# Issuing each weight block's load one block ahead in a streaming-encoder layer on eight cores

## The chip, the cores and the metric

The kernel runs on one Trainium2 chip as one program on 8 cores. Each core gets one half of one of four prompt sequences and two of sixteen short sample sequences; the cores exchange nothing. The metric is the device time of the slowest core in microseconds (us), as the median over runs.

## The reference, cut to what matters

One transformer-like layer with two parallel head groups. For every token of width 1024:

```python
h = rms_norm(x) * (1 + scale1) + shift1
z = h @ w_in                                  # 1024 x 3584, seven blocks of 512 columns
qa, ka, va, qr, kr, vr, gr = split(z)         # blocks 0, 1, 2, 3, 4, 5, 6
qa, ka = rms_norm per 64 columns
qr, kr = rotate(qr, pos), rotate(kr, pos)     # rotary tables
oa  = diff_attention(qa, ka, va)              # 4 heads, two softmax maps, 64-token causal chunks
orr = retention_scan(qr, kr, vr) * silu(gr)   # 4 heads, recurrent state
x = x + gate1 * (concat(oa, orr) @ w_out)     # two blocks of 512 columns
h2 = rms_norm(x) * (1 + scale2) + shift2
x = x + gate2 * ((silu(h2 @ w_gate) * (h2 @ w_up)) @ w_down)   # 11 blocks up, 6 blocks down
```

Outputs are the new `x` for prompt and sample, the normalised keys, the values and the final retention states. The prompt has 8192 tokens per sequence, the sample 32 tokens on top of a cache of 2048.

## The kernel before, in words

The program is written out by Python. Each operation is appended to the list of its engine together with the buffers that it reads and writes; the semaphores that an instruction waits for follow from these. Nothing is reordered: each engine, and each of the two queues that issue transfers, works through its list in program order. All loads into on-chip memory come from the SP queue (helper `ld`), all stores to HBM and all casting loads from the POOL queue (`stq`). So a load on SP that has to wait for its buffer holds up every load behind it.

The prompt is done in eight steps of two tiles of 512 tokens: the **foreign** tile, which the core only needs for keys, values and state, and the **own** tile, for which it computes everything. `in_proj` multiplies a tile by blocks of `w_in`. For the foreign tile the blocks are 1, 2, 4, 5, here called F1, F2, F4, F5; for the own tile they are 1, 2, 0, 4, 5, 3, 6, here called O1, O2, O0, O4, O5, O3, O6. A block has four groups of 8 matmuls (128 tokens each) that go to four PSUM banks in turn, and each group is then read out by VectorE (DVE) or ScalarE (ACT): blocks 0 and 1 by a norm (`qknorm`), blocks 3 and 4 by a rotation (`rope`, six DVE operations), blocks 2 and 5 by copies that alternate between ACT and DVE. After F1's matmuls the hook `own_norm` loads the own tile's `x` (`s_xo`) and normalises it: ACT squares and sums, DVE writes `s_xn`. A block's transposes are put off until after the next block's matmuls.

Weights go through `wring`, a ring of three slots of 1 MB. `load_w` takes the next slot, and its load waits for the last matmul that read the slot's former block (three blocks earlier). In the source the load stands at the head of its own block. Rotary tables (`s_rt`, two buffers of 512 KB) are loaded in blocks 3 and 4, one per group, so the third and the fourth of such a block wait for the first and the second `rope` of that block. Attention loads keys and values (`s_ktb`, `s_vsb`) in pairs of 128 KB through two buffers.

A step goes: F blocks, store of the foreign keys and values, state update, transposes of the own tile, O blocks (`kp`, `vp` are stored from one buffer each, four times), retention, attention over all earlier tiles (so later steps are longer), output projection (`Wo`), norm, feed-forward (`Wgu` eleven blocks, `Wd` six), with the next foreign tile's norm hooked into it. The last stage does the sample with 64 tokens.

Weights arrive in 32-bit floats and are cast once into 16-bit scratch in HBM by the POOL queue: `Wi` at the very start, `Wo`, `Wgu`, `Wd` in the middle of the first step (`prepass_rest`).

Of the kernel before, what the change touches and what calls it, by code (L numbers as in the profile page):

```python
# [294 lines left out]
def build_program(n_steps=NT // 2, do_sample=True, cut=0):  # L295
    def chk(n):
        if cut == n:
            raise _StopBuild()
# [32 lines left out]
    rope_d = din("rope", [NT, TT, 4, 256])  # L331
# [16 lines left out]
    Wi = dscr("Wi", [7, 128, 8, 512], BF16)  # L348
# [156 lines left out]
    def load_w(src, nk, ncol, rkeys):  # L505
        view, key = wslot(nk, ncol)
        ld(view, src, r=rkeys, w=[key])
        return view, key

    def setup():  # L510
        ld(kc[:], kc_d[:], w=["kc"])
        ld(dco[:], dco_d[:], w=["dco"])
# [213 lines left out]
                else:  # L726
                    act(dest[:, h, 0:T], tbb[:, half * 512:half * 512 + T], AF.Copy, [tk], [(dname, h)])

    def in_proj(rows, nsub, own, sample, tabsrc, tile_i, hook_after_first=None):
        T = rows * nsub  # L730
        hk_ = hT_keys(sample)
        cbs = (1, 2, 0, 4, 5, 3, 6) if own else (1, 2, 4, 5)
        pending = [None]

        def flush():
            if pending[0] is not None:
                pending[0]()
                pending[0] = None
        for cb in cbs:
            W, wkey = load_w(Wi[cb], 8, 512, [("Wi", cb)])  # L740
            if cb == 6:
                for e in range(4):
                    acc, ak = next_acc()
                    for k in range(8):
                        mm(acc[:, 0:T], W[:, k, e * 128:(e + 1) * 128], hT[:, k, 0:T], k == 0, k == 7, [wkey] + hk_, [ak])
                    act(sgT[:, e, 0:T], acc[:, 0:T], AF.Silu, [ak], [("sgT", e)])
                flush()
                continue
            for s in range(nsub):
                acc, ak = next_acc()  # L750
                for k in range(8):
                    mm(acc[0:rows, :], hT[:, k, s * rows:(s + 1) * rows], W[:, k, :], k == 0, k == 7, [wkey] + hk_, [ak])
                chk(31)
                if cb == 0:
                    qknorm(acc, ak, rows, 0, tokb[0:rows, s, :], ("tokb", s), s % 2)
                elif cb == 1:
                    if own:
                        kfv = kf[0:rows, 0, :]
                        qknorm(acc, ak, rows, 64, kfv, "kf", s % 2)
                        if sample:  # L760
                            out_ops.append(stq(ksm[:, :], kfv, r=["kf"]))
                        else:
                            out_ops.append(stq(kp[tile_i, s * 128:(s + 1) * 128, :], kfv, r=["kf"]))
                        act(tokb[0:rows, s, :], kfv, AF.Copy, ["kf"], [("tokb", s)])
                    else:
                        qknorm(acc, ak, rows, 64, tokb[0:rows, s, :], ("tokb", s), s % 2)
                elif cb == 2:
                    if own:
                        vfv = vf[0:rows, 0, :]
                        act(vfv, acc[0:rows, :], AF.Copy, [ak], ["vf"])  # L770
                        if sample:
                            out_ops.append(stq(vsm[:, :], vfv, r=["vf"]))
                        else:
                            out_ops.append(stq(vp[tile_i, s * 128:(s + 1) * 128, :], vfv, r=["vf"]))
                        cp(vst[0:rows, s, :], vfv, ["vf"], [("vst", s)])
                    else:
                        evac(vst[0:rows, s, :], acc[0:rows, :], [ak], [("vst", s)])
                elif cb in (3, 4):
                    rs_ = s % 2
                    ld(rt[0:rows, rs_], tabsrc(s), w=[("rt", rs_)])  # L780
                    if cb == 3:
                        rope(acc, ak, rows, rt[0:rows, rs_, 0, :], rt[0:rows, rs_, 1, :], ("rt", rs_), tokb[0:rows, s, :], ("tokb", s), s % 2)
                    else:
                        rope(acc, ak, rows, rt[0:rows, rs_, 2, :], rt[0:rows, rs_, 3, :], ("rt", rs_), ke[0:rows, s, :], ("ke", s), s % 2)
                elif cb == 5:
                    evac(vR[0:rows, s, :], acc[0:rows, :], [ak], [("vR", s)])
            if hook_after_first is not None and cb == cbs[0]:
                hook_after_first()
            flush()
            if cb == 0:  # L790
                pending[0] = lambda: transp_heads(tokb, lambda s: [("tokb", s)], rows, nsub, qAT, "qAT", split=True)
            elif cb == 1:
                pending[0] = lambda: transp_heads(tokb, lambda s: [("tokb", s)], rows, nsub, kst, "kst")
            elif cb == 3:
                pending[0] = lambda: transp_heads(tokb, lambda s: [("tokb", s)], rows, nsub, qdT, "qdT")
            elif cb == 4 and own:
                pending[0] = lambda: transp_heads(ke, lambda s: [("ke", s)], rows, nsub, keT, "keT")
        flush()
# [164 lines left out]
    def out_proj(rows, nsub, xviews, xkeys):  # L963
        okeys = [("oT", i) for i in range(8)]
        for cb2 in range(2):
            W, wkey = load_w(Wo[cb2], 8, 512, [("Wo", cb2)])
            for s in range(nsub):
                acc, ak = next_acc()
                for k in range(8):
                    mm(acc[0:rows, :], oT[:, k, s * rows:(s + 1) * rows], W[:, k, :], k == 0, k == 7, [wkey] + okeys, [ak])  # L970
                t = et[0:rows, (cb2 * nsub + s) % 2, :]
                tkey = f"et{(cb2 * nsub + s) % 2}"
                tt(t, acc[0:rows, :], gate1b[0:rows, cb2 * 512:(cb2 + 1) * 512], ALU.mult, [ak, ("gate", 0, cb2)], [tkey])
                xv = xviews[s][:, cb2 * 512:(cb2 + 1) * 512]
                tt(xv, t, xv, ALU.add, [tkey, xkeys[s]], [xkeys[s]])

    def ffn(rows, nsub, xviews, xkeys, sample, store, gb_hooks=None, mid_hook=None):
        T = rows * nsub
        hk_ = hT_keys(sample)
        for gb in range(11):  # L980
            W, wkey = load_w(Wgu[gb], 8, 512, [("Wgu", gb, 0), ("Wgu", gb, 1)])
            if gb_hooks is not None and gb in gb_hooks:
                gb_hooks[gb]()
            for fc in range(2):
                pg, pgk = next_acc()
                pu, puk = next_acc()
                for k in range(8):
                    mm(pg[:, 0:T], W[:, k, fc * 128:(fc + 1) * 128], hT[:, k, 0:T], k == 0, k == 7, [wkey] + hk_, [pgk])
                for k in range(8):
                    mm(pu[:, 0:T], W[:, k, 256 + fc * 128:256 + (fc + 1) * 128], hT[:, k, 0:T], k == 0, k == 7, [wkey] + hk_, [puk])  # L990
                sgi = (2 * gb + fc) % 2
                sg = lg[:, sgi, 0:T]
                act(sg, pg[:, 0:T], AF.Silu, [pgk], [("lg", sgi)])
                tt(ffT[:, 2 * gb + fc, 0:T], pu[:, 0:T], sg, ALU.mult, [puk, ("lg", sgi)], [("ffT", 2 * gb + fc)])
# [5 lines left out]
        for half in range(2):  # L1000
            accs = [next_acc() for s in range(nsub)]
            for bi, (k0, k1) in enumerate(((0, 8), (8, 16), (16, 22))):
                W, wkey = load_w(Wd[half][:, k0:k1, :], k1 - k0, 512, [("Wd", half, bi)])
                for s in range(nsub):
                    acc, ak = accs[s]
                    for kk in range(k0, k1):
                        mm(acc[0:rows, :], ffT[:, kk, s * rows:(s + 1) * rows], W[:, kk - k0, :], kk == 0, kk == NKF - 1, [wkey] + fkeys, [ak])
# [33 lines left out]
    try:  # L1041
# [14 lines left out]
        for step in range(n_steps):  # L1056
# [5 lines left out]
                    ld(xviews[s], xs[slotO, s * 128:(s + 1) * 128, :], w=[xkeys[s]])  # L1062
                norm_part(xviews, xkeys, 128, [0, 1, 2, 3], 0)
            chk(1)
            in_proj(128, 4, False, False, lambda s, slot=slotF: rope_d[slot, s * 128:(s + 1) * 128], step, hook_after_first=own_norm)
            chk(2)
            store_kv(slotF)
            pu, pk = psb[7], PS(7)
# [21 lines left out]
            for h in range(4):  # L1090
                ts(tmpS[:, h, :], S[:, h, :], dco[:, 8 + h:9 + h], None, ALU.mult, None, ["S", "dco"], [("tmpS", h)])
                stt(tmpS[:, h, :], Uf[:, h, :], dco[:, 16 + h:17 + h], tmpS[:, h, :], ALU.mult, ALU.add, ["Uf", "dco", ("tmpS", h)], [("tmpS", h)])
                stt(S[:, h, :], pu[:, h * 128:(h + 1) * 128], dco[:, 12 + h:13 + h], tmpS[:, h, :], ALU.mult, ALU.add, [pk, "dco", ("tmpS", h)], ["S"])
            chk(6)
            for h in range(4):
                attention(0, 512, prompt_units(step, h), h)
            chk(7)
# [7 lines left out]
            if step + 1 < n_steps:  # L1105
                nslot = 2 * (step + 1)
                ffn(128, 4, xviews, xkeys, False, store,
                    gb_hooks={1 + 2 * s_: (lambda nslot=nslot, s_=s_: foreign_sub(nslot, s_)) for s_ in range(4)}, mid_hook=foreign_part2)
            else:
                ffn(128, 4, xviews, xkeys, False, store)  # L1110
        out_ops.append(stq(rp[:].rearrange("h d e -> d h e"), S[:, :, :], r=["S"]))
# [135 lines left out]
```

How the kernel before makes its waits and increments, by code:

```python
        def run_engine(e, h):  # L151
            seen = {}
            nwait = 0
            for o in prog.ops[e]:
                need = {}
                for d in o.deps:
                    if (not d.is_dma) and d.eng == e and e == "pe" and not o.is_dma:
                        continue
                    k = d.sem
                    if d.val > seen.get(k, 0) and d.val > need.get(k, 0):
                        need[k] = d.val
                for k, v in need.items():
                    h.wait_ge(sem_h[k], v)
                    seen[k] = v
                    nwait += 1
                ins = o.fn(h)
                if o.is_dma:
                    ins.then_inc(sem_h[o.sem], 16)
                elif o.signal:
                    ins.then_inc(sem_h[o.sem], 1)
            if e == "sp":
                for k, v in cnt.items():
                    h.wait_ge(sem_h[k], v)
            prog.stats["n_wait"][e] = nwait
```

## Time and profile before

| | |
|---|---|
| median of 2 runs | 5278.8 us (5278.3 to 5279.2) |
| profiled execution, time | 5300.7 us |
| its span on the slowest core (core 5) | 5299.1 us |
| spans of the eight cores | 5268.3 to 5299.1 us |
| mean granted TensorE clock of the cores | 0.888 to 0.897 |
| TensorE (PE) matmul busy | 4040.6 us, 76% |
| ACT busy | 2372.2 us, 45% |
| DVE busy | 1278.3 us, 24% |

How to read it: busy time is the sum of instruction durations on the slowest core. A granted clock of 1.0 is 2.4 GHz and 0.5 is 1.2 GHz. A wait is put down to whichever of the awaited events came last; a load's time is from issue to landing. The timelines of two engines have the same zero, so that a row of SP can be laid beside a row of PE.

### The profile page before, as it was taken

To read this page: it belongs to the slowest core of one execution; us is meant where nothing else is said; L and a number is where in the kernel's file an instruction comes from. 1 tells how busy PE (TensorE), PEld (TensorE's weight loads), DVE (VectorE), ACT (ScalarE), POOL (GpSimd) and SP (SyncE) were. 2 spreads that over 40 slices of the span, in tenths; PEclk is the share of its full clock that TensorE was granted. 3 is DMA by queue.
4 is the path that set the end of the run, shared out by engine and by line. 5 is a ranking of instruction groups with operands and counts; after the bars stand their busy time and mean duration, and the time that the engine had idled before them with its cause. 6 is when DMAs were issued, how large, how long until landed. Compare 5 with 4: busy or idle time off the path is not lost.

```text
span 5299.1 us, 62757 instructions; the slowest of 8 cores (5268.3 to 5299.1 us)
## 1 busy us (share of the span) xinstructions
PE 4040.6 (76%) x19438; PEld 1734.8 (33%) x19438; DVE 1278.3 (24%) x2668; ACT 2372.2 (45%) x3571; POOL 201.5 (4%) x289
## 2 busy tenths in 40 slices
PE   1557966886888688967898688985898966989854
PEld 1223422332333233422333233332333422333323
DVE  0233242233223311242023311133101242001111
ACT  0225324523652366335752367622677324776033
POOL 1010010000000000010000000000000010000000
PEclk8778987998899899988999889998899988999956
DMA  9689551244125412351125411254111452112545
GB/s 120 151 152 142 166 150 46 94 165 131 29 92 172 130 32 68 136 178 44 40 93 170 130 32 41 90 170 139 31 42 59 139 159 72 42 40 66 144 118 180
DMA packets 248993, 556.28 MB, mean 105 GB/s; under 512 B 38660, under 2 KB 180171, under 8 KB 216928
## 3 DMA queue, kind: packets, MB, share of 16 engines
q1 hardware_dynamic: 156240, 444.51, 25.7%
q0 software_dynamic: 92432, 107.77, 11.8%
q8 instruction: 168, 2.75, 0.2%
q14 instruction: 153, 1.25, 0.1%
HBM read 548.22 MB, written 86.78 MB: 120 GB/s over the span
## 4 chain that ended last, share of the span: by engine, by line
PE 59%; DMA 12%; ACT 12%; DVE 9%; issue 8%; DVEq 0%; ACTq 0%; SPq 0%; POOL 0%; POOLq 0%
PE psall L433 58%; DMA s_wring<-Wi 4%; DVE s_et L448 4%; ACT s_Pm L444 3%; ACT s_hT L444 2%; ACT s_et L444 2%; ACT s_lg L444 1%; DMA vp<-s_vf 1%; DMA kp<-s_kf 1%; DVE s_stat L688 1%; DMA Wi<-w_in 1%; ACT s_sqb L444 1%; ACT s_stat L444 1%; DMA y<-s_xo 1%; PE psall L440 1%
## 5 line engine op out<-in xcount | busy, mean ns | idle before, releaser
L444 ACT ACTIVATE s_Pm<-psall,s_cols 128x1024 bf16<-128x1024 f32 (+4 forms) x1332 | 1223.8, 926 | 417.9 <-PE psall L433 376.1
L433 PE MATMUL psall<-s_wring,s_hT 128*128 128x512 bf16 (+1 forms) x2608 | 680.7, 422 | 421.3 <-DMA s_wring<-Wi 202.3
L433 PE MATMUL psall<-s_Pm,s_vsb 128*128 128x512 bf16 (+4 forms) x2560 | 729.0, 354 | 201.9 <-ACT s_Pm L444 145.6
L433 PE MATMUL psall<-s_hT,s_wring 128*128 128x512 bf16 (+1 forms) x3456 | 725.4, 376 | 110.0 <-DMA s_wring<-Wi 67.2
L433 PE MATMUL psall<-s_qAT,s_ktb 128*128 128x512 bf16 (+4 forms) x2560 | 701.6, 359 | 28.7 <-ACT s_et L444 26.0
L433 PE MATMUL psall<-s_Pm,s_onesb 128*128 128x512 bf16 (+5 forms) x2576 | 702.4, 354 | 20.9 <-DVE s_S L456 19.0
L433 PEld LDWEIGHTS psall<-s_wring,s_hT 128*128 128x128 bf16 (+1 forms) x2608 | 269.3, 106 | 811.1 <-issue 586.4
L433 PEld LDWEIGHTS psall<-s_hT,s_wring 128*128 128x128 bf16 x3456 | 327.4, 103 | 505.9 <-issue 175.3
L433 PEld LDWEIGHTS psall<-s_Pm,s_vsb 128*128 128x128 bf16 x2560 | 186.5, 97 | 675.0 <-issue 659.7
L456 DVE SCALAR_TENSOR_TENSOR s_lg<-psall,s_G 128x128 f32<-128x128 f32 x120 | 31.5, 292 | 1415.5 <-PE psall L433 1414.9
L433 PEld LDWEIGHTS psall<-s_qAT,s_ktb 128*128 128x128 bf16 x2560 | 243.0, 99 | 306.4 <-issue 51.8
L433 PEld LDWEIGHTS psall<-s_Pm,s_onesb 128*128 128x128 bf16 (+1 forms) x2576 | 240.2, 98 | 272.8 <-issue 37.7
L444 ACT ACTIVATE s_lg<-psall 128x512 f32<-128x512 f32 (+2 forms) x238 | 144.4, 607 | 409.6 <-PE psall L433 408.9
L433 PE MATMUL psall<-s_wring,s_ffT 128*128 128x512 bf16 (+1 forms) x1452 | 322.0, 384 | 5.7 <-DMA s_wring<-Wd 4.6
L448 DVE TENSOR_TENSOR s_ffT<-psall,s_lg 128x512 bf16<-128x512 f32 (+1 forms) x198 | 126.7, 640 | 543.5 <-PE psall L433 410.2
L433 PE MATMUL psall<-s_warmb,s_onesb 128*128 128x512 bf16 x1008 | 224.6, 380 | 0.0
L444 ACT ACT_TABLE_LOAD x94 | 120.6, 1283 | 201.3 <-PE psall L433 184.1
L444 ACT ACTIVATE s_et<-psall 128x512 f32<-128x512 f32 (+2 forms) x106 | 59.1, 558 | 323.7 <-PE psall L433 279.9
L433 PEld LDWEIGHTS psall<-s_wring,s_ffT 128*128 128x128 bf16 (+1 forms) x1452 | 143.5, 99 | 180.9 <-issue 16.8
L448 DVE TENSOR_TENSOR s_et<-psall,s_rt 128x256 f32<-128x256 f32 (+1 forms) x392 | 165.6, 422 | 129.2 <-DMA s_rt<-rope 73.7
L444 ACT ACTIVATE s_Pm<-s_lg 128x128 bf16<-128x128 f32 (+3 forms) x408 | 138.5, 350 | 82.7 <-DVE s_lg L456 52.9
L444 ACT ACTIVATE s_hT<-psall,s_modc 128x512 bf16<-128x512 bf16 (+1 forms) x224 | 141.7, 727 | 72.8 <-PE psall L440 71.3
(158 smaller groups left out, 2632.8 us busy)
## 6 DMA issues: line engine op xcount, KB each, us to landing
s_wring<-Wgu SPq DMA_DIRECT2D x99, 1024.0 KB, 5.9
s_wring<-Wi SPq DMA_DIRECT2D x95, 1024.0 KB, 7.8
s_rt<-rope SPq DMA_DIRECT2D x96, 512.0 KB, 5.9
s_ktb<-KT SPq DMA_DIRECT2D x288, 128.0 KB, 2.0
s_vsb<-VS SPq DMA_DIRECT2D x288, 128.0 KB, 2.0
s_wring<-Wd SPq DMA_DIRECT2D x36, 1024.0 KB, 4.9
s_wring<-Wo SPq DMA_DIRECT2D x18, 1024.0 KB, 7.8
s_wring<-w_ada POOLq DMA_DIRECT2D x16, 1024.0 KB, 12.4
```

The lines of the kernel that those rows point to most:

```text
L433: return P.op("pe", lambda e: e.matmul(out, lhsT=lhsT, rhs=rhs, start=start, stop=stop), reads=r, writes=w)
L440: return P.op("pe", lambda e: e.transpose(out, in_, ident), reads=r, writes=w)
L444: return P.op("act", lambda e: e.activation(out=out, in_=in_, func=func, bias=bias, scale=scale), reads=r, writes=w)
L448: return P.op(eng, lambda e: e.tensor_tensor(out=out, in0=in0, in1=in1, op=op), reads=r, writes=w)
L456: return P.op("dve", lambda e: e.scalar_tensor_tensor(out=out, in0=in0, scalar=scalar, in1=in1, op0=op0, op1=op1), reads=r, writes=w)
L688: P.op("dve", lambda e: e.tensor_reduce(out=stat[0:rows, sc:sc + 8], in_=sq.rearrange("p (g j) -> p g j", g=8), axis=AX.X, op=ALU.add), re ...
```

## The change

`load_w` is split in two. A table `WSRC` names the source of each weight block; `prefetch(name)` issues the load into the next ring slot and keeps the view in `pf`, and `get_w(name)` hands that view out, or loads on the spot if there is none. In `in_proj` and `ffn` each block first gets its own weights and then prefetches the next block's, before any other load of the block; the last block prefetches the first of what comes next where the caller names it (`next_w`). Before attention the three blocks `Wo` 0, `Wo` 1 and `Wgu` 0 are prefetched. The ring keeps its three slots, and the engines PE, DVE, ACT and POOL keep their instructions and their order.

```diff
+    def prefetch(name):
+        if name not in pf:
+            pf[name] = load_w(*WSRC[name])
+
+    def get_w(name):
+        if name in pf:
+            return pf.pop(name)
+        return load_w(*WSRC[name])
...
-        for cb in cbs:
-            W, wkey = load_w(Wi[cb], 8, 512, [("Wi", cb)])
+        for ci, cb in enumerate(cbs):
+            W, wkey = get_w(("Wi", cb))
+            if ci + 1 < len(cbs):
+                prefetch(("Wi", cbs[ci + 1]))
+            elif next_w is not None:
+                prefetch(next_w)
...
-            W, wkey = load_w(Wo[cb2], 8, 512, [("Wo", cb2)])
+            W, wkey = get_w(("Wo", cb2))
...
-            W, wkey = load_w(Wgu[gb], 8, 512, [("Wgu", gb, 0), ("Wgu", gb, 1)])
+            W, wkey = get_w(("Wgu", gb))
+            prefetch(("Wgu", gb + 1) if gb + 1 < 11 else ("Wd", 0, 0))
...
-                W, wkey = load_w(Wd[half][:, k0:k1, :], k1 - k0, 512, [("Wd", half, bi)])
+                W, wkey = get_w(("Wd", half, bi))
+                nxt = ("Wd", half, bi + 1) if bi < 2 else (("Wd", 1, 0) if half == 0 else next_w)
+                if nxt is not None:
+                    prefetch(nxt)
...
+            prefetch(("Wo", 0))
+            prefetch(("Wo", 1))
+            prefetch(("Wgu", 0))
             for h in range(4):
                 attention(0, 512, prompt_units(step, h), h)
```

Where this moves loads is seen in the SP queue. Its list for the first step, from F1 to the first loads of attention, before the change (`s_wring<-Wi` is a block of `w_in`, `s_xo<-xs` the own tile, `s_rt<-rope` a rotary table; the third row from the end is O6's load):

```order
L462 DMA s_wring<-Wi 128x4096
L462 DMA s_xo<-xs 128x1024 x4
L462 DMA s_wring<-Wi 128x4096 x2
L462 DMA s_rt<-rope 128x1024 x4
L462 DMA s_wring<-Wi 128x4096 x5
L462 DMA s_rt<-rope 128x1024 x4
L462 DMA s_wring<-Wi 128x4096 x2
L462 DMA s_rt<-rope 128x1024 x4
L462 DMA s_wring<-Wi 128x4096
L462 DMA s_ktb<-KT 128x512
L462 DMA s_vsb<-VS 128x512
```

The same stretch of the SP queue with the change:

```order
L462 DMA s_wring<-Wi 128x4096 x2
L462 DMA s_xo<-xs 128x1024 x4
L462 DMA s_wring<-Wi 128x4096 x2
L462 DMA s_rt<-rope 128x1024 x4
L462 DMA s_wring<-Wi 128x4096 x5
L462 DMA s_rt<-rope 128x1024 x4
L462 DMA s_wring<-Wi 128x4096 x2
L462 DMA s_rt<-rope 128x1024 x4
L462 DMA s_wring<-Wo 128x4096 x2
L462 DMA s_wring<-Wgu 128x4096
L462 DMA s_ktb<-KT 128x512
L462 DMA s_vsb<-VS 128x512
```

Every weight load has moved up by one place among the weight loads: F2 now stands ahead of the four `x` loads, F5 ahead of F4's four tables, O5 ahead of O4's, and O6 ahead of O3's. The three blocks that are needed after attention stand ahead of its first key and value loads.

## Rows read from the trace of the kernel before

**Rows 1.** The page: the span and the engines' busy times.

```profile
span 5299.1 us, 62757 instructions; the slowest of 8 cores (5268.3 to 5299.1 us)
PE 4040.6 (76%) x19438; PEld 1734.8 (33%) x19438; DVE 1278.3 (24%) x2668; ACT 2372.2 (45%) x3571; POOL 201.5 (4%) x289
```

**Rows 2.** Waits of PE, whole span: who for whom, us in total, times, longest.

```profile
PE psall L433 <- DMA s_wring<-Wi: 269.5, 25, 18.6
PE psall L433 <- DVE s_et L448: 195.2, 84, 12.6
...
PE psall L433 <- DMA s_wring<-Wgu: 15.0, 8, 4.2
```

**Rows 3.** Timeline of PE, fifth step, F1 to F5: start, us, idle before.

```profile
2871.82 7.07 PE L433 MATMUL psall<-s_wring,s_hT 128*128 128x512 bf16 x32
2890.35 8.79 PE L433 MATMUL psall<-s_wring,s_hT 128*128 128x512 bf16 x32 [11.46 <-DMA s_wring<-Wi]
...
2899.87 7.07 PE L433 MATMUL psall<-s_wring,s_hT 128*128 128x512 bf16 x32
2916.86 9.18 PE L433 MATMUL psall<-s_wring,s_hT 128*128 128x512 bf16 x32 [9.93 <-DMA s_wring<-Wi]
```

**Rows 4.** Timeline of PE, same step, end of O4 to the transposes after O6.

```profile
2986.29 1.06 PE L440 MATMUL psall<-s_identb,s_tokb 128*128 128x128 bf16 x16
2999.75 8.70 PE L433 MATMUL psall<-s_wring,s_hT 128*128 128x512 bf16 x32 [12.40 <-DMA s_wring<-Wi]
...
3009.18 7.07 PE L433 MATMUL psall<-s_wring,s_hT 128*128 128x512 bf16 x32
3024.95 9.74 PE L433 MATMUL psall<-s_hT,s_wring 128*128 128x512 bf16 x32 [8.70 <-DMA s_wring<-Wi]
3034.53 1.06 PE L440 MATMUL psall<-s_identb,s_tokb 128*128 128x128 bf16 x16
```

**Rows 5.** Timeline of the SP queue, same step: first issue, us to the last, count.

```profile
2873.37 8.61 SPq L462 DMA_DIRECT2D s_xo<-xs  x4
2882.13 0.80 SPq L462 DMA_DIRECT2D s_wring<-Wi  x2
2882.98 24.86 SPq L462 DMA_DIRECT2D s_rt<-rope  x4
2907.99 35.57 SPq L462 DMA_DIRECT2D s_wring<-Wi  x5
2943.71 46.97 SPq L462 DMA_DIRECT2D s_rt<-rope  x4
2990.83 0.80 SPq L462 DMA_DIRECT2D s_wring<-Wi  x2
```

**Rows 6.** Timeline of DVE, same step: F1's last norm, own norm, O4's first ropes.

```profile
2887.10 0.69 DVE L448 TENSOR_TENSOR s_tokb<-s_et,s_gfull 128x512 bf16<-128x512 f32 x1
2891.75 2.74 DVE L452 TENSOR_SCALAR s_xn<-s_xo,s_stat 128x1024 bf16<-128x1024 f32 x4 [3.96 <-ACT s_stat L444]
...
2985.14 0.95 DVE L448 TENSOR_TENSOR s_et<-psall,s_rt 128x256 f32<-128x256 f32 x2
...
2987.92 0.95 DVE L448 TENSOR_TENSOR s_et<-psall,s_rt 128x256 f32<-128x256 f32 x2
```

**Rows 7.** Transfers of the whole span: issuer, count, KB each, median us to landing.

```profile
s_rt<-rope SPq DMA_DIRECT2D x96, 512.0 KB, 5.9
...
vp<-s_vf POOLq DMA_DIRECT2D x32, 256.0 KB, 2.3
```

**Rows 8.** Chain of waits, fifth step: the second of O1's key stores.

```profile
2946.47 7.26 DMA kp<-s_kf
```

**Rows 9.** First step: PE's waits up to 470 us; POOL's casting of Wgu.

```profile
PE psall L433 <- DMA s_wring<-Wi: 34.0, 2, 18.6
...
345.27 0.83 POOL L465 DMA_DIRECT2D Wgu<-wu  x1 [4.30 <-DMA Wgu<-wu]
```

**Rows 10.** Fifth step by stretch: us, busy times, granted clock, DMA share, GB/s.

```profile
2934.00:2987.00 53.00, 36.12 (x157) 15.07 (x158) 19.52 (x32) 14.82 (x37) 11.79 (x18) 0.86 0.43 111
```

More of the change, by code:

```diff
@@ L508, in load_w @@
         return view, key
+    pf = {}
+    WSRC = {}
+    for cb_ in range(7):
+        WSRC[("Wi", cb_)] = (Wi[cb_], 8, 512, [("Wi", cb_)])
+    for cb_ in range(2):
+        WSRC[("Wo", cb_)] = (Wo[cb_], 8, 512, [("Wo", cb_)])
+    for gb_ in range(11):
+        WSRC[("Wgu", gb_)] = (Wgu[gb_], 8, 512, [("Wgu", gb_, 0), ("Wgu", gb_, 1)])
+    for half_ in range(2):
+        for bi_, (k0_, k1_) in enumerate(((0, 8), (8, 16), (16, 22))):
+            WSRC[("Wd", half_, bi_)] = (Wd[half_][:, k0_:k1_, :], k1_ - k0_, 512, [("Wd", half_, bi_)])
+    def prefetch(name):
[5 more added lines that the diff above has]
+        return load_w(*WSRC[name])
     def setup():
@@ L727, in transp_heads, with in_proj @@
                     act(dest[:, h, 0:T], tbb[:, half * 512:half * 512 + T], AF.Copy, [tk], [(dname, h)])
-    def in_proj(rows, nsub, own, sample, tabsrc, tile_i, hook_after_first=None):
+    def in_proj(rows, nsub, own, sample, tabsrc, tile_i, hook_after_first=None, next_w=None):
         T = rows * nsub
@@ L975, in out_proj, with ffn @@
                 tt(xv, t, xv, ALU.add, [tkey, xkeys[s]], [xkeys[s]])
-    def ffn(rows, nsub, xviews, xkeys, sample, store, gb_hooks=None, mid_hook=None):
+    def ffn(rows, nsub, xviews, xkeys, sample, store, gb_hooks=None, mid_hook=None, next_w=None):
         T = rows * nsub
@@ L1064, in build_program @@
             chk(1)
-            in_proj(128, 4, False, False, lambda s, slot=slotF: rope_d[slot, s * 128:(s + 1) * 128], step, hook_after_first=own_norm)
+            in_proj(128, 4, False, False, lambda s, slot=slotF: rope_d[slot, s * 128:(s + 1) * 128], step, hook_after_first=own_norm, next_w=("Wi", 1))
             chk(2)
@@ L1107, in build_program @@
                 ffn(128, 4, xviews, xkeys, False, store,
-                    gb_hooks={1 + 2 * s_: (lambda nslot=nslot, s_=s_: foreign_sub(nslot, s_)) for s_ in range(4)}, mid_hook=foreign_part2)
+                    gb_hooks={1 + 2 * s_: (lambda nslot=nslot, s_=s_: foreign_sub(nslot, s_)) for s_ in range(4)}, mid_hook=foreign_part2,
+                    next_w=("Wi", 1))
             else:
```

## The prediction

> **What bounds the kernel now.** I began with the page's busy times. PE works 76% of the 5299.1 us span and no other engine more than 45% [rows 1], so the end is set by PE and by what PE waits for. The second view, PE's waits, names the largest single cause: blocks of `w_in` that have not landed, 269.5 us in 25 waits; the blocks of the feed-forward cost 15.0 us in 8 [rows 2]. The third view, PE's timeline of one step, shows where: after F1 PE stands idle for 11.46 us before F2, and after F4 for 9.93 us before F5 [rows 3]; in the own tile 12.40 us before O5 and 8.70 us before O6 [rows 4]. That is 42.5 us per step, 340 us over eight steps; it exceeds the 269.5 us because the waits view puts some of these gaps down to another event that ended about as late.
>
> The fourth view, the SP queue beside PE, gives the reason. F2's load is issued at 2882.13, right behind the last of the four `x` loads, which came at 2873.37 + 8.61 = 2882.0 [rows 5]; PE had been ready since 2871.82 + 7.07 = 2878.9 [rows 3]. F5's load goes out at 2907.99, directly behind the fourth table load, and O5's at 2990.83 in the same way [rows 5]. The ring had a free slot in each case; the load stood behind others in an in-order queue. So the gaps are queueing, and the change addresses just that.
>
> **F2.** The change takes F2's load past four `x` loads. Its ring slot is freed when the second-to-last `Wd` block is done, 24 matmuls (5.3 us at F1's pace of 7.07 us for 32) before 2871.8, so at 2866.5. F2's load takes 2882.13 to about 2890.0 now, 8 us; moved, it lands by 2875, before F1 is done. PE then meets the next limit, the four PSUM banks. F1's last bank is read by the DVE operation just ahead of 2887.10 [rows 6], so F2's fourth group starts at 2887.0 and ends at 2888.8, where it ended at 2890.35 + 8.79 = 2899.1: 10 us gained, not yet kept.
>
> **F4 and F5.** F2's copies stand on ACT behind the own norm, and on DVE behind the four `s_xn` operations, 2891.75 to 2894.5 [rows 6]; neither moves, since the `x` loads wait for the last step's `y` stores. The copies take about 0.7 us each, so F4's banks come free at 2892.3 (ACT), 2895.2 and 2895.9 (DVE), and F4 ends at 2900.6 instead of 2906.9. A rope takes 2987.92 - 2985.14 = 2.78 us [rows 6]. The first two ropes of F4 run 2895.9 to 2901.4. The third needs the table whose load is issued when the first is nearly done (2898.3) and lands 5.9 us later [rows 7]: 2904.2 to 2907.0. The fourth runs 2907.0 to 2909.8. F5's last group waits for its bank and ends at 2911.2 instead of 2916.86 + 9.18 = 2926.0 [rows 3]. **Gain 15 us**, out of gaps of 21.4: the rest turns into waits for banks and ropes. The two tables of F4 now stand behind F5 instead of F2, the same 1 MB, so I cost that at nothing.
>
> **O5, O3, O6.** O4's matmuls end at 2986.3 [rows 4]. With O5's weights there, its groups follow O4's ropes: two end by 2990.7, the third starts when its table lands, about 2993, and the fourth ends at about 2999. O5 ends at 3000.5 instead of 3008.4. O3's load is issued where it is now, right after the fourth table, and is first of its pair, so it lands 8.7 us after 2990.83 like O5's does today (PE starts at 2999.75): in time for 3001.4. O3's own ropes then run 3003.1 to 3008.7, the third 3011.8 to 3014.6, the fourth 3014.6 to 3017.4, and O6, which now only waits for banks, ends at 3018.8 instead of 3024.95 + 9.74 = 3034.7 [rows 4]. **Gain 16 us**, out of gaps of 21.1.
>
> **What gets later.** (1) O4's first two tables now stand behind O5's load, which needs O2's slot: not before O2's last matmul, some 18 us later than now (2943.71 [rows 5]). Three loads (2 MB) then land within 8 us; the first rope needs them at 2985.1 [rows 6], 15 us of slack, so cost nothing. But this 2 MB now falls on the `vp` stores that O2 waits for. A store of that size lands in 2.3 us [rows 7]; the `kp` store that runs into such a burst today took 7.26 us [rows 8]. One `vp` store pays +4 to +5 us, one `kp` store gets 3 us back: net 1 us lost per step; bounds: 2 us gained to 10 us lost, if all of three stores pay. (2) Key and value loads stand behind `Wgu` 0, which waits for O6's matmuls; after that come more than 30 us of retention before attention, against some 15 us for 3 MB. Hidden; if retention were not there it would be exposed. (3) `Wo` and `Wgu` 0 were never waited for in the prompt steps: no gain. (4) The foreign `x` loads in the feed-forward move behind one more `Wgu` block, up to 7 us later, before an ACT operation that PE does not wait for: nothing. (5) The sample stage keeps its load order but for its tables: nothing, plus or minus 3 us.
>
> **Clock.** After each gap PE needs 8.7 to 9.7 us for 32 matmuls that take 7.07 without one [rows 3, 4]: 1.7 to 2.7 us of low clock. My replay assumes the high level throughout; the new, shorter bank waits may keep some of the loss. Only the last group of a stretch counts, the others hide under ropes: 0 to 7 us per step. O1 to O4 have such short bank waits today and are granted 0.86 [rows 10], close to the high level, so I take 1.5.
>
> A rule of the Trainium skill speaks against me here (TensorE: Matmul & The Clock Gate, "A second HAM failure mode: psum-queue depth-cycling"): brief idle times between groups that cycle through PSUM banks can send the clock back and forth. By that rule the sum would be that of the second rival below; the 0.86 bears it out in part.
>
> **Sum.** 15 + 16 - 1 = 30 us in each of seven steps: 210. In the first step, whose two own gaps are 34.0 us [rows 9] and in which transfers are slowed by the casting traffic, I take 20 for the own tile and 6 for the foreign one: 26. Its attention loads must now wait for `Wgu` 0 to be cast, done by 345.3 [rows 9], before O6 ends, so nothing is added. 236 - 8 x 1.5 = **224 us**. The profiled execution took 5300.7 us and would come to 5077; the median of the runs shown is 0.4% lower, 5278.8, so I forecast **5055 us**.
>
> **Rivals.** *Stores collide (slower).* Place: the single-buffered `kp` and `vp` stores of O1 and O2 and the `y` stores, about eight per step on the chain. They share the transfer engines with the loads that now come sooner. If each took 7.3 us instead of 2.3, that is 40 us per step, 320 in all, against 236: 5363 us, and with the `x` loads and tables slowed in the same way 5390. It decides only if the loss passes 30 us per step. Against it: the loads are the same bytes, only one burst moves, and the `kp` store is relieved. The Trainium skill (DMA: Bandwidth & Descriptors, "Issuing engines are not separate DMA queues") says that transfers of all issuers interleave on the same 16 engines; the 7.26 us store agrees. 2%.
>
> *Low clock.* If six groups of 8 per step run at 1.2 GHz where they count, each costs 7.07 / 4 = 1.8 us more: 86 us in all instead of 12, 5129 us. For it: F2 to F5 will be nothing but groups with waits between. 17%.
>
> *The ropes and copies take nearly all.* If table loads land in 9 us rather than 5.9 because a weight block is in front, each of three rope blocks loses 6 us: 18 x 8 = 144, and 5199 us, within 2%. For it: DVE is already PE's second largest releaser, 195.2 us [rows 2]. Against: the order of bytes around the tables hardly changes. 6%. That the change does nothing at all (the loads stay queued) the order of SP rules out, but for 1%.
>
> *Everything comes back.* All 340 us plus 1.7 us of clock at 32 restarts, 394 us: 4885. The ropes forbid it; part of it (gain over 280) 10%.
>
> **How the numbers follow.** The forecast, a gain of 180 to 280 (4999 to 5099), has 64%. Low clock adds 5099 to 5150. From 4995 to 5135 lie the forecast and most of the low-clock case, 79%. A measurement of this kernel can tell about 2% from no change, 106 us, so faster means below 5173: 64 + 17 + 10 = 91%; within 2%: 7%; slower: 2%.
>
> **What would show it.** The gaps of 8 to 12 us before F2, F5, O5 and O6 vanish from PE's timeline; waits on `Wi` fall from 269.5 us to under 40; waits of PE on DVE `s_et` and on ACT copies rise by some 60 to 120 us. SP issues F2 before the `x` loads. F1's start to F5's end shrinks from 54.2 to about 39 us, O5's idle plus O5 to O6 from 48.4 to about 33. Attention and feed-forward keep their length. I am wrong if table loads or `vp` stores lengthen by more than 3 us each, if gaps of the old size remain before any of the four blocks, or if the granted clock around the F blocks falls below today's.

## The result, and the profile after

The change makes the kernel faster: the ratio of its time to that of the kernel before, from runs of both in turn, is 0.9625 (95% interval 0.9598 to 0.9652). On the 5278.8 us of the runs shown ahead of the prediction that is 5081 us (5067 to 5095), a gain of 198 us (184 to 212). The profiled executions took 5300.7 and 5087.8 us, 213 us apart. The medians of all eleven runs of the changed kernel, 5093.1 us, and of ten of the kernel before, 5399.6 us, hold executions in which the cores of one die got a lower clock, and the ratio and all times below leave these out. The forecast was 5055 us, a gain of 224.

The page of the changed kernel, its head and PE's own line, where [rows 1] stood:

```profile
span 5086.1 us, 62404 instructions; the slowest of 8 cores (5042.2 to 5086.1 us)
PE 4000.3 (79%) x19093; PEld 1725.2 (34%) x19438; DVE 1274.5 (25%) x2668; ACT 2374.2 (47%) x3571; POOL 202.3 (4%) x289
```

PE's waits over the whole span, where [rows 2] stood (who for whom, us in total, times, longest):

```profile
PE psall L433 <- DVE s_et L448: 251.7, 158, 9.5
...
PE psall L433 <- ACT s_vf L444: 51.7, 16, 6.5
...
PE psall L433 <- ACT s_vst L444: 20.2, 8, 2.9
...
PE psall L433 <- DMA s_wring<-Wgu: 11.2, 8, 3.1
```

The 269.5 us on `Wi` have no row any more. The waits on DVE's ropes and norms went from 195.2 us in 84 pieces to 251.7 in 158: few long gaps have become many short ones. The waits on ACT's copies, `s_vf` and `s_vst`, went from 23.6 and 2.5 us to 51.7 and 20.2. The stretch from F1 to F5 of the fifth step on PE (start, us, what, idle before), where [rows 3] stood, on the slowest core, whose fifth step is here at 2754. (The name stands for the step that the program numbers 5, counting from 0, here and in the rows ahead of the prediction: the one at 2872 us before and at 2754 now. It is the sixth; the first starts at 203 and 206 us.)

```profile
2754.10 8.80 PE L433 MATMUL psall<-s_wring,s_hT 128*128 128x512 bf16 x40
2763.61 1.67 PE L433 MATMUL psall<-s_wring,s_hT 128*128 128x512 bf16 x7 [0.71 <-DVE s_et L448]
2766.28 1.89 PE L433 MATMUL psall<-s_wring,s_hT 128*128 128x512 bf16 x8 [1.00 <-DVE s_et L448]
2769.16 1.89 PE L433 MATMUL psall<-s_wring,s_hT 128*128 128x512 bf16 x8 [0.99 <-DVE s_et L448]
...
2774.35 1.89 PE L433 MATMUL psall<-s_wring,s_hT 128*128 128x512 bf16 x8 [2.41 <-ACT s_vst L444]
2777.26 8.79 PE L433 MATMUL psall<-s_wring,s_hT 128*128 128x512 bf16 x39 [1.03 <-DVE s_vst L459]
2787.58 1.89 PE L433 MATMUL psall<-s_wring,s_hT 128*128 128x512 bf16 x8 [1.52 <-DVE s_et L448]
2790.37 1.89 PE L433 MATMUL psall<-s_wring,s_hT 128*128 128x512 bf16 x7 [0.90 <-DVE s_et L448]
```

F1 to F5 takes 2754.1 to 2792.3, 38.2 us; it was 54.2. No gap is longer than 2.4 us. F2's groups come 2.9 us apart, as fast as the norm of F1 frees their banks; F4 then waits for the copies on ACT and DVE. The same stretch on the SP queue (first issue, us to the last, count), where [rows 5] stood:

```profile
2749.22 0.32 SPq L462 DMA_DIRECT2D s_wring<-Wi  x1
2756.36 8.13 SPq L462 DMA_DIRECT2D s_xo<-xs  x4
2764.64 0.80 SPq L462 DMA_DIRECT2D s_wring<-Wi  x2
2765.49 18.04 SPq L462 DMA_DIRECT2D s_rt<-rope  x4
```

F2's load is out at 2749.22, before the `x` loads. In the own tile, from the transposes after O4 to those after O6, where [rows 4] stood:

```profile
2851.83 1.06 PE L440 MATMUL psall<-s_identb,s_tokb 128*128 128x128 bf16 x16
2853.38 1.67 PE L433 MATMUL psall<-s_wring,s_hT 128*128 128x512 bf16 x7 [0.49 <-DVE s_et L448]
2855.95 1.89 PE L433 MATMUL psall<-s_wring,s_hT 128*128 128x512 bf16 x8 [0.90 <-DVE s_et L448]
2862.20 6.54 PE L433 MATMUL psall<-s_wring,s_hT 128*128 128x512 bf16 x16 [4.36 <-DVE s_et L448]
2868.58 1.06 PE L440 MATMUL psall<-s_identb,s_ke 128*128 128x128 bf16 x16
2869.47 7.07 PE L433 MATMUL psall<-s_wring,s_hT 128*128 128x512 bf16 x31
2876.38 3.62 PE L433 MATMUL psall<-s_hT,s_wring 128*128 128x512 bf16 x16
2880.86 1.89 PE L433 MATMUL psall<-s_hT,s_wring 128*128 128x512 bf16 x7 [0.86 <-DVE s_et L448]
2884.10 1.89 PE L433 MATMUL psall<-s_hT,s_wring 128*128 128x512 bf16 x8 [1.36 <-DVE s_et L448]
2885.83 1.06 PE L440 MATMUL psall<-s_identb,s_tokb 128*128 128x128 bf16 x16
```

34.0 us instead of 48.2. One gap of 4.36 us is left, the rope of the third group, and the 16 matmuls after it take 6.54 us instead of 3.62: the granted clock was 0.54 there. The chain of waits of this step names what that rope waited for, the third rotary table, and shows the store that got longer, the second of O2's:

```profile
2826.44 5.72 DMA vp<-s_vf
...
2853.10 6.51 DMA s_rt<-rope
```

To see all eight steps at once I took the start and end of each stretch from PE's timeline, on each of the eight cores, and added up the eight steps; the table gives the median of the cores in us. This table is the yardstick for the experiments.

| stretch | before | changed | forecast for the change |
|---|---|---|---|
| F1 to F5 | 431 | 315 | -111 |
| O1 to O4 | 409 | 422 | +8 |
| O4's end to O6's end | 380 | 268 | -132 |
| state update and transposes, retention | 354 | 356 | 0 |
| attention | 2018 | 2011 | 0 |
| output projection, norm | 229 | 227 | 0 |
| up-projections | 658 | 658 | 0 |
| of these, the first step's | 83 | 86 | 0 |
| down-projections | 305 | 305 | 0 |

Two more views. The granted clock by stretch, fifth step (F1 to F5, O1 to O4, O4 to O6: us, busy times, clock, DMA share, GB/s), first before:

```profile
2871.80:2926.00 54.20, 32.81 (x148) 14.31 (x146) 24.62 (x46) 14.81 (x31) 5.29 (x8) 0.81 0.72 230
2934.00:2986.30 52.30, 35.42 (x145) 14.37 (x146) 18.87 (x31) 14.82 (x36) 11.79 (x18) 0.86 0.43 112
2986.30:3034.50 48.20, 27.10 (x129) 12.09 (x128) 20.05 (x48) 11.06 (x18) 0.00 (x0) 0.75 0.47 152
```

and changed:

```profile
2754.10:2792.10 38.00, 29.33 (x143) 12.99 (x145) 24.10 (x46) 14.55 (x31) 5.28 (x8) 1.00 0.87 300
2800.60:2851.80 51.20, 34.46 (x141) 14.05 (x143) 18.83 (x31) 14.84 (x36) 11.84 (x18) 0.87 0.49 135
2851.80:2885.80 34.00, 25.92 (x126) 11.60 (x128) 19.88 (x48) 10.96 (x18) 0.00 (x0) 0.90 0.72 230
```

In this step the F blocks run wholly at the high level, 1.00 instead of 0.81, and the transfer engines move 300 GB/s there instead of 230: the same bytes in less time. It is the best of the slowest core's eight steps; over all steps, as the median of the cores, the granted clock went from 0.81 to 0.95 in F1 to F5, from 0.78 to 0.92 from O4 to O6, and fell from 0.88 to 0.86 in O1 to O4. And the waits for the stores of O1 and O2, whole span, first before, then changed:

```profile
ACT s_vf L444 <- DMA vp<-s_vf: 73.6, 23, 4.6
DVE s_kf L448 <- DMA kp<-s_kf: 28.0, 8, 4.5
```

```profile
ACT s_vf L444 <- DMA vp<-s_vf: 105.8, 23, 7.8
DVE s_kf L448 <- DMA kp<-s_kf: 2.2, 4, 1.0
```

### The profile page after: what moved, and what is told of

The parts are those of the page before. It is cut to its first block, busy times and chain, and to the rows that moved or that the text cites. A ratio compares the mean times of both kernels' runs of the same rounds, so it can differ in the third digit from the quotient of the medians.

```text
span 5086.1 us, 62404 instructions; the slowest of 8 cores (5042.2 to 5086.1 us)
## 1 busy us (share of the span) xinstructions
PE 4000.3 (79%) x19093; PEld 1725.2 (34%) x19438; DVE 1274.5 (25%) x2668; ACT 2374.2 (47%) x3571; POOL 202.3 (4%) x289
## 4 chain that ended last, share of the span: by engine, by line
PE 56%; ACT 13%; DMA 11%; DVE 10%; issue 9%; DVEq 0%; ACTq 0%; SPq 0%; POOL 0%; POOLq 0%
PE psall L433 56%; DVE s_et L448 4%; ACT s_Pm L444 4%; DMA s_rt<-rope 4%; ACT s_et L444 2%; ACT s_hT L444 2%; DMA vp<-s_vf 2%; ACT s_lg L444 1%; DVE s_stat L709 1%; DMA s_browb<-b_ada 1%; ACT s_stat L444 1%; DMA Wi<-w_in 1%; ACT s_sqb L444 1%; PE psall L440 1%; DMA urd<-s_et 1%
## 5 line engine op out<-in xcount | busy, mean ns | idle before, releaser
L433 PE MATMUL psall<-s_Pm,s_vsb 128*128 128x512 bf16 (+3 forms) x2520 | 723.8, 356 | 209.2 <-ACT s_Pm L444 153.7
L433 PE MATMUL psall<-s_wring,s_hT 128*128 128x512 bf16 (+1 forms) x2544 | 665.1, 415 | 272.2 <-DVE s_et L448 168.2
L433 PE MATMUL psall<-s_hT,s_wring 128*128 128x512 bf16 (+1 forms) x3387 | 707.3, 370 | 71.3 <-DVE s_et L448 28.5
L433 PE MATMUL psall<-s_Pm,s_onesb 128*128 128x512 bf16 (+4 forms) x2534 | 695.5, 354 | 23.5 <-DVE s_S L456 18.8
L448 DVE TENSOR_TENSOR s_et<-psall,s_rt 128x256 f32<-128x256 f32 (+1 forms) x392 | 165.6, 422 | 113.1 <-DMA s_rt<-rope 71.3
```

What stands on the lines that cost most here:

```text
L433: return P.op("pe", lambda e: e.matmul(out, lhsT=lhsT, rhs=rhs, start=start, stop=stop), reads=r, writes=w)
L448: return P.op(eng, lambda e: e.tensor_tensor(out=out, in0=in0, in1=in1, op=op), reads=r, writes=w)
```

## The experiments

All times are against the kernel before, whose runs lay between 5269.9 and 5287.7 us in the three series. A ratio is given where there were runs enough for an interval; elsewhere the single times are. The stretches are medians of the cores of one profiled execution each.

**Only the input projection.** All prefetches outside `in_proj` are taken out again.

```diff
-            prefetch(("Wgu", gb + 1) if gb + 1 < 11 else ("Wd", 0, 0))
...
-                nxt = ("Wd", half, bi + 1) if bi < 2 else (("Wd", 1, 0) if half == 0 else next_w)
-                if nxt is not None:
-                    prefetch(nxt)
...
-            prefetch(("Wo", 0))
-            prefetch(("Wo", 1))
-            prefetch(("Wgu", 0))
```

> Only the prefetches inside the input projection (and the one of O1 at the end of the F blocks) are kept; output projection and feed-forward load as before. Queueing theory: everything the change gained came from F2, F5, O5 and O6, so this keeps all of it: ratio 0.96 to before, F blocks about 39 us per step instead of 54, O4 to O6 about 33 instead of 48; the first step's up-projection, which grew from 83.7 to 90.3 us with the whole change, is back at 84. Rival (part of the gain comes from the early Wo and Wgu loads): ratio 0.97 to 0.98.

Measured: 5070.0 and 5074.2 us beside 5269.9 and 5281.4 of before, so about 0.961. F 315, O4 to O6 268, as with the whole change; the first up-projection 82. The whole gain is in the input projection.

**Only the rest.** The other half of the change: no prefetch in `in_proj`.

```diff
-            if ci + 1 < len(cbs):
-                prefetch(("Wi", cbs[ci + 1]))
-            elif next_w is not None:
-                prefetch(next_w)
```

> Only the prefetches of Wo, Wgu and Wd are kept, none inside the input projection. Queueing theory: no gain, ratio 0.998 to 1.003, and the first step's up-projection at 90 us. Rival: ratio 0.98 to 0.99, because these blocks are then never late.

Measured: 5273.0 us, a single run, where before had 5269.9 and 5281.4. No gain, as the queueing theory says. Its first up-projection took 82 us on six of the eight cores and not 90 (98 on the other two, at a granted clock of 0.81): that expectation failed. It starts at 510 to 529 us in this kernel and at 491 to 509 in the changed one, where ACT's wait for the `x` load is 4.2 to 8.7 us. So the late `x` load seems to need the earlier start as well; the experiment with the x load first comes back to it.

**F2 alone.** Only this one load is moved, ahead of the `x` loads.

```diff
-            if ci + 1 < len(cbs):
-                prefetch(("Wi", cbs[ci + 1]))
-            elif next_w is not None:
-                prefetch(next_w)
+            if ci == 0 and not own:
+                prefetch(("Wi", cbs[ci + 1]))
```

> Only F2 is prefetched, ahead of the four x loads. Queueing theory: the 11 to 12 us gap before F2 goes, but F2's copies still stand behind the own norm, and F5's load still stands behind F4's tables, so only about 6 us per step are kept: F blocks 48 us instead of 54, 45 us in all, ratio 0.991. Rival (the gaps are independent and each is kept whole): 11 us per step, ratio 0.984.

Measured: 5224.2, 5225.6 and 5228.6 us, 0.991 of the 5269.9 and 5281.4 beside them. F1 to F5 373 us in eight steps, 46.6 each, everything else as before; that is 58 us less in the traces and 50 in the times. PE and the SP queue, fifth step:

```profile
2850.59 5.34 PE L433 MATMUL psall<-s_wring,s_hT 128*128 128x512 bf16 x23 [1.03 <-DVE s_vst L459]
2866.31 8.81 PE L433 MATMUL psall<-s_wring,s_hT 128*128 128x512 bf16 x31 [10.38 <-DMA s_wring<-Wi]
```

```profile
2838.67 18.18 SPq L462 DMA_DIRECT2D s_rt<-rope  x4
2857.01 18.57 SPq L462 DMA_DIRECT2D s_wring<-Wi  x4
```

F4 runs early, and F5 waits 10.38 us as before: its load goes out at 2857.01, behind the fourth table. Each gap has its own cause in the queue, and of F2's gap only 7 us per step are kept, near the 6 that the order of the copies behind the own norm gave ahead.

**No prefetch, four table buffers.** The kernel before, with room for all four tables of a block, so that no table load waits for a rope.

```diff
+    ffTf = ffT.bitcast(F32)
...
+    def rt_buf(s):
+        if s < 2:
+            return rt[:, s], [("rt", s)]
+        c = 4 * (s - 2)
+        return ffTf[:, c:c + 4, :], [("rt", s)] + [("ffT", c + i) for i in range(4)]
...
-                    rs_ = s % 2
-                    ld(rt[0:rows, rs_], tabsrc(s), w=[("rt", rs_)])
+                    tv, tkk = rt_buf(s)
+                    tv = tv[0:rows]
+                    ld(tv, tabsrc(s), w=[tkk])
```

> The kernel before, with no prefetch at all, but with four buffers for the rotary tables instead of two (the third and fourth lie in the feed-forward's buffer, which is idle then). No table load waits for a rope any more, so no weight load behind one is held up. Queueing theory: the gaps before F5, O5 and O6 go without any weight load being moved, that before F2 stays: F blocks 54 to about 45 us, O4 to O6 48 to about 30, ratio 0.96. Rival (the gaps come from bandwidth, 1 MB simply takes 8 us and more next to the tables): the gaps stay or grow, ratio 0.99 to 1.01.

Measured: 5052.9 us in a single run, the profiled one, 35 us less than the changed kernel's. F1 to F5 342, O1 to O4 427, O4 to O6 223. PE, fifth step (this kernel's helpers stand one line lower):

```profile
2740.68 9.50 PE L434 MATMUL psall<-s_wring,s_hT 128*128 128x512 bf16 x32 [12.79 <-ACT s_stat L445]
...
2750.91 12.37 PE L434 MATMUL psall<-s_wring,s_hT 128*128 128x512 bf16 x56
2764.19 1.89 PE L434 MATMUL psall<-s_wring,s_hT 128*128 128x512 bf16 x8 [0.90 <-DVE s_et L449]
...
2841.07 7.07 PE L434 MATMUL psall<-s_wring,s_hT 128*128 128x512 bf16 x32
2847.98 5.34 PE L434 MATMUL psall<-s_hT,s_wring 128*128 128x512 bf16 x24
```

On the SP queue of the same step the block that F2 needs goes out behind the `x` loads:

```profile
2722.64 9.36 SPq L463 DMA_DIRECT2D s_xo<-xs  x4
2732.15 0.81 SPq L463 DMA_DIRECT2D s_wring<-Wi  x2
```

F2's gap stays, 12.79 us. The view puts it down to an ACT operation that ended about as late; PE was ready at 2727.9, and F2's load was only issued at 2732.15. The three other gaps are gone though no weight load was moved. That rules out that 1 MB simply came too late for want of bandwidth. The gaps before F5, O5 and O6 came from table loads that waited for ropes in the same queue.

**Four table buffers in the changed kernel.** The same edit on top of the change.

> The changed kernel with four table buffers instead of two. Theory (what is left in the F blocks and from O4 to O6 is the third and fourth table, each loaded only when a rope frees a buffer): F blocks 39 to about 37 us, O4 to O6 33 to about 26, some 70 us in all, 5015 us. Rival (DVE's ropes and copies are the limit, tables or not): within 15 us of the changed kernel. Rival 2 (four tables at once, 2 MB, delay the weight blocks behind them): O4 to O6 stays at 33.

Measured: 5021.4 us in the profiled execution and 5065.0 in another, ratio 0.9555 (0.9451 to 0.9659), an interval too wide to tell the gain over the change from nothing. The stretches do tell: F 293, O4 to O6 219, together 71 us less than changed, at the expected sizes. But O1 to O4 rose from 422 to 434: with four tables at once the first `vp` store is longer still, as this kernel's chain of waits shows in its fifth step.

```profile
2767.26 8.39 DMA vp<-s_vf
```

**Four kf and vf buffers in the changed kernel.** No key or value store holds up the next group.

```diff
+    def st_buf(which, s):
+        if s == 0:
+            return (kf if which == "kf" else vf)[:, 0, :], [which]
+        c = (8 if which == "kf" else 14) + 2 * (s - 1)
+        return ffTf[:, c:c + 2, :].rearrange("p a b -> p (a b)"), [(which, s), ("ffT", c), ("ffT", c + 1)]
...
-                        kfv = kf[0:rows, 0, :]
+                        kfv, kk = st_buf("kf", s)
...
-                        vfv = vf[0:rows, 0, :]
+                        vfv, vk = st_buf("vf", s)
```

> The changed kernel with four buffers each for the key and value rows that are stored (kf, vf) instead of one. Theory (O1 and O2 wait for their own stores, and more so now that a table burst falls on the vp stores): O1 to O4 falls from 52 us per step to about 36, 130 us in all, about 4960 us. Rival (the norms of O1 and O0 on ACT and DVE set the pace, the stores only fill their gaps): O1 to O4 falls by under 5 us per step, 5050 us or more.

Measured: 4980.5 to 5008.3 us in four runs, ratio 0.9463 (0.9426 to 0.9500). O1 to O4 309 instead of 422, more than 14 us per step; O4 to O6 gives 25 us back (293). DVE's waits for rotary tables rose from 71.3 to 92.3 us on the slowest core; that tables and stores now meet there fits, and with four tables as well the loss is gone (217 below), but no run separates the two. The expected 4960 us was missed by 20 to 48: O1 to O4 fell by 113 us and not by some 130, and these 25 came on top. The single-buffered stores, not the norms, set the pace of O1 and O2.

**Tables first.** In blocks 3 and 4 the next weight block is issued after the first two tables.

```diff
             if ci + 1 < len(cbs):
-                prefetch(("Wi", cbs[ci + 1]))
+                if cb not in (3, 4) or nsub < 4:
+                    prefetch(("Wi", cbs[ci + 1]))
...
                     ld(rt[0:rows, rs_], tabsrc(s), w=[("rt", rs_)])
+                    if s == 1:
+                        prefetch(("Wi", cbs[ci + 1]))
```

> The changed kernel, but in blocks 3 and 4 the next weight block is issued after the block's first two tables instead of before them (still ahead of the third and fourth). Theory (a weight block ahead of the first two tables delays them, and pushes O4's onto the vp stores): first tables of F4 land within 8 us instead of 12, vp stores back to under 4 us, O1 to O4 52 to about 50 us, F blocks and O4 to O6 about 1 us shorter each; 20 to 30 us in all, 5060 us. Rival (the order among loads issued within a microsecond does not matter): within 8 us of 5087.

Measured: 5068.6 and 5082.1 us, ratio 0.9616 (0.9569 to 0.9662), and 5118.0 us in the profiled execution, which that ratio leaves out. The times alone do not decide between 5060 and 5087. The stretches do: F 317, O1 to O4 420, O4 to O6 268, where the theory wanted some 16 us off O1 to O4 and 8 off each of the others. My theory fell, and the sum is as the rival had it. The waits of this kernel say why:

```profile
ACT s_vf L444 <- DMA vp<-s_vf: 87.3, 24, 6.2
DVE s_kf L448 <- DMA kp<-s_kf: 29.2, 9, 4.8
```

The `vp` stores got 18 us back and the `kp` stores lost 27: the burst of loads falls on one kind of store or on the other.

**The x load first.** In the feed-forward the next foreign tile's `x` load is issued ahead of the `Wgu` block.

```diff
-            prefetch(("Wgu", gb + 1) if gb + 1 < 11 else ("Wd", 0, 0))
             if gb_hooks is not None and gb in gb_hooks:
                 gb_hooks[gb]()
+            prefetch(("Wgu", gb + 1) if gb + 1 < 11 else ("Wd", 0, 0))
```

> The changed kernel, but in the feed-forward the next foreign tile's x load is issued ahead of the prefetched Wgu block instead of behind it. Theory (in the first step the x load, one block later and beside the casting of Wd, came 8.7 us late and held ACT and then PE): the first step's up-projection is back from 90 to 84 us, the others stay, 6 us in all. Rival (the up-projection is longer for another reason, such as the clock): 90 us as before.

Measured: 5076.8 and 5079.8 us, ratio 0.9621 (0.9585 to 0.9657): too small to see in the time. In the traces it shows. ACT in the first step's up-projection, changed kernel (start, us, idle before):

```profile
533.41 1.06 ACT L445 ACTIVATE s_Pm<-s_xf 128x1024 bf16<-128x1024 f32 x1 [8.69 <-DMA s_xf<-xs]
```

and with the x load first:

```profile
523.43 1.06 ACT L445 ACTIVATE s_Pm<-s_xf 128x1024 bf16<-128x1024 f32 x1 [1.24 <-DMA s_xf<-xs]
```

On the slowest core the stretch went from 90.3 to 81.9 us; over the cores the median went from 86 to 82. It took 82 us too with the early start but no `Wgu` prefetch (only the input projection), and 91 with four table buffers, where it starts earlier still, at 474 to 486 us, and that wait is 7.6 to 9.6 us. So my "nothing" for this move was wrong in the first step, by 3 to 4 us, and right in the other seven.

**All three, and all three without the prefetches.** The first kernel is the changed one with four table buffers, four kf and vf buffers and the `x` load first. The second has the same buffers but, of the prefetches, only that of F2.

> The changed kernel with four table buffers, four kf and vf buffers, and the x load ahead of the Wgu block. If the three effects add up: 5087 less 66 (tables) less 92 (kf, vf) less 8 (x load) = 4921 us, ratio 0.932. F blocks 37 us, O1 to O4 38, O4 to O6 27, first up-projection 82. If they get in each other's way (the tables, the weight blocks and eight stores now all fall into one stretch): 4960 us or more, with O4 to O6 above 32.

> The kernel before with four table buffers, four kf and vf buffers, and a single prefetch, that of F2 ahead of the x loads. Theory (with four table buffers no load in the queue waits for a rope, so the order of the weight blocks no longer matters except behind the x loads): as fast as the whole change with the same buffers, within 15 us of it. Rival (the prefetches still pay, because the weight blocks stand behind 2 MB of tables): 30 us or more slower than it, with gaps before F5 or O5.

Measured: 4898.7, 4901.8 and 4908.6 us for the first, ratio 0.9293 (0.9275 to 0.9311), the fastest kernel with an interval, better than both given kernels; 4896.9 and 4903.1 us for the second, beside 5273.8 to 5280.6 of before. The gains add up, to a little more than the 4921 us of the plain sum. With these buffers the other prefetches are worth nothing in total, as expected; by stretch they bring 12 us from O4 to O6 and lose 21 in retention.

| us, eight steps, median of cores | F1 to F5 | O1 to O4 | O4 to O6 | retention |
|---|---|---|---|---|
| before | 431 | 409 | 380 | 289 |
| changed | 315 | 422 | 268 | 291 |
| F2 alone | 373 | 409 | 381 | 289 |
| before, four tables | 342 | 427 | 223 | 290 |
| changed, four tables | 293 | 434 | 219 | 291 |
| changed, four kf and vf | 316 | 309 | 293 | 291 |
| changed, tables first | 317 | 420 | 268 | 291 |
| all | 293 | 307 | 217 | 311 |
| buffers and F2 only | 292 | 307 | 229 | 290 |

In the kernel with all of it a new wait appears in retention, 311 instead of 290 us: the stores and the casting loads of the sample's cache are now on the chain. It does not come from the buffers alone, for the kernel with buffers and F2 only has 290. The chain of waits in the fifth step:

```profile
2684.41 9.80 DMA vp<-s_vf
2695.99 10.89 DMA VS<-s_vst
2707.45 15.04 DMA VSs<-cv
2723.04 9.87 DMA s_vst<-ck
```

## Why the prediction was right or wrong

**Right: the cause and the place.** The gaps were queueing on SP and not bandwidth. One half of the change brings all of the gain and the other half none, F2 alone removes its own gap and leaves F5's, and four table buffers remove F5's, O5's and O6's without any weight load being moved. The four gaps are gone, `Wi` has left PE's waits, waits on DVE `s_et` rose by 57 us and those on ACT's copies by 46, 103 together, all as listed ahead.

**Right: F2 to F5.** 15 us per step were replayed and 6 for the first, 111 in all; 116 were measured. In the fifth step F2's groups are bound by the norm, F4's by the copies behind the own norm and F5's by the ropes, in that order, and the stretch lasts 38.2 us where the replay gave 39.4.

**Wrong in size: O4 to O6, the step that failed.** The term was "Gain 16 us" in seven steps and 20 us in the first; 14 and 13 were measured. The step "the third starts when its table lands, about 2993, and the fourth ends at about 2999. O5 ends at 3000.5" failed. It put the third table 6.7 us after O4's end; in the changed kernel it landed at 2853.10 + 6.51 = 2859.6, 7.8 us after it, and then the clock was low: the last 16 matmuls of O5 took 6.54 us instead of 3.62. O5 ended 16.8 us after O4 where 14.2 were replayed. Over the eight steps the stretch gained 112 us, not 132. Four table buffers bring it to 219, at a granted clock of 1.00 instead of 0.92, so it was the tables that held it. The 20 us of the first step had no replay behind them at all. I had costed clock losses apart, 12 us in all, so the sum is off by less than this term.

**Nearly right: the stores. Missed: the clock beside them.** "One `vp` store pays +4 to +5 us, one `kp` store gets 3 us back", +8 us in all: the waits on `vp` rose by 32 us and those on `kp` fell by 26, +6 for ACT and DVE. The whole stretch O1 to O4 grew by 13. Of these, 4 are idle time of PE (from 128 to 132, mean of the cores), and 9 are time in which it ran its matmuls (from 281 to 290): the granted clock fell from 0.88 to 0.86. My clock term looked only at the new waits from F2 to O6 and took O1 to O4 as unchanged. The Trainium skill (DMA: Bandwidth & Descriptors, "Issuing engines are not separate DMA queues") says that transfers of all issuers share the same engines; the store of 5.72 us agrees, and the burst only moves from one store to the other.

**Wrong: an `x` load costed at nothing.** It holds ACT 8.69 us in the first step, where the casting of weights still loads the transfer engines. Its price is 3 to 4 us, and moving it back removes it.

**The sum, and the reference point.** Against the forecast terms F2 to F5 brought 5 us more, O1 to O4 cost 5 more, O4 to O6 brought 20 less, and the 12 us set aside for the clock are already inside the stretches: 116 - 13 + 112 give 215 us from the traces, 9 less than the 224 forecast, and the profiled pair is 213 apart. The repeated runs say 198 (184 to 212), so the forecast of 5055 us was 26 us low against 5081. Part of the 17 us between 215 and 198 is that the profiled execution before was a long one, 5300.7 us where the two runs beside it took 5278.8; the changed kernel's, 5087.8, is close to its 5081. In the experiment with only the rest, whose F blocks have the old order, F1 to F5 took 416 to 430 us on four cores, against 424 to 437 on the eight here. The measured 5081 us lie inside the stated range of 4995 to 5135. Set on the later median of 5399.6 us, though, the same ratio gives 5197 us, outside it. A forecast in us holds only for the reference time that it was tied to. As a ratio it was 0.958, against 0.9625 (0.9598 to 0.9652): the direction and the mechanism were right, the size a little too large.

**The rivals.** *Stores collide:* the mechanism is there, its size is 6 us of waits on ACT and DVE and 4 on PE, not 320. The single-buffered stores are a far larger item, 113 us in the changed kernel, but the change did not make them so: with four tables O1 to O4 takes 427 us without any prefetch, and 307 once the stores have buffers and F2 is prefetched. *Low clock:* not borne out from F2 to F5, where the granted clock rose from 0.81 to 0.95, nor from O4 to O6, where it rose from 0.78 to 0.92; shorter gaps in place of long ones gave clock back. In part it held in O1 to O4, 9 us. The rule of the Trainium skill on idle times between PSUM banks (TensorE: Matmul & The Clock Gate, "A second HAM failure mode: psum-queue depth-cycling") did not hold for the fifth step's F blocks, 1.00 with idle times of 0.7 to 2.4 us between groups; the one fall from O4 to O6 of that step came after a gap of 4.36 us. *Ropes and copies take nearly all:* they took a part, 49 us from O4 to O6 and 22 in the F blocks by the experiment with four tables, not 144. *Everything comes back:* no.

## What to carry to other kernels

When a load is late, look first at what stands ahead of it in its queue and what that is waiting for; in a queue like this one, worked through in order, a small load with too few buffers holds up every large one behind it. Giving the small loads their buffers did more here (5052.9 us) than moving the large loads ahead of them (5087.8 us), and with both the move was worth nothing beyond one load. Replay the stretch with the buffers and banks that come next before counting a gap as gain: 42.5 us of gaps per step were worth 27 in the traces. And give a stretch that you take as unchanged its own look at the clock: O1 to O4 lost 9 us to it.

## What the runs showed of the hardware that was not expected

The transfer engines of one core moved 300 GB/s over the 38 us of the F blocks, up from 230, and the tables' median time to landing rose only from 5.9 to 6.2 us. A store of 256 KB, 2.3 us by the median, took 5.72, 8.39 and 9.80 us next to bursts of loads, in the changed kernel, with four tables and in the kernel with all of it. In the fifth step's F blocks the clock kept its high level for 38 us through gaps of 0.7 to 2.4 us, and between O4 and O6 it was low after one of 4.36 us. That is no sharp line: in O1 to O4 of the same step a group of 8 matmuls took 3.27 us instead of 1.89 after a gap of 2.64 us. What decides between them the runs do not show.
